# Differential attention in a two-block transformer kernel: rotation and lambda placed beside the projection, head norms in the attention loop, two weight slots filled ahead

## The chip, the cores and the metric

The kernel runs on one core of a Trainium2 chip. The metric is the device time of one execution in microseconds (us), as the median of several runs. All arithmetic here is in 32-bit floating point, but for the gather matmuls of the experts, which run on bf16 parts.

## The reference

Two transformer blocks of two layers each work on 256 tokens of width 1024, with 256 context tokens beside them. The part that the change touches is layer 1 of the first block, and the expert layers of the same block.

```python
# mixer_c: differential attention, 8 heads, each of two components of width 64
q, k, v = split(concat(ux, uc) @ c_w_qkv)          # 1024 columns each; q of the 256 tokens alone
q, k = rope(q), rope(k)                            # the 256 tokens of x; context rows are not rotated
lam = exp(sum(lq1 * lk1)) - exp(sum(lq2 * lk2)) + lam_init        # one per head
a = softmax(q1 @ k1.T / 8) - lam * softmax(q2 @ k2.T / 8)
o = a @ v                                          # 128 columns per head
o = o * rsqrt(mean(o * o) + eps) * c_subln_g * (1 - lam_init)     # head norm
y = o @ c_w_out
# hier_moe: 32 experts of width 512, the best two of a group per token
y = sum_over_two(weight * (silu(z @ w_gate[e]) * (z @ w_up[e])) @ w_down[e])
```

## The kernel before

The whole program is written out as a row of stages. A stage (`with self.stage()`) gives each engine its own list of instructions, and the next stage begins on every engine once all have come to the end of their lists. Semaphores order the engines inside a stage. An issued DMA does not hold up a stage's end unless an engine waits for it.

**Weights.** One plan lists all weight pieces in the order of their use. They go through a ring of six slots of 1 MB in SBUF, and SyncE (SP) issues a piece as soon as the slot's last user is done (`feed`, L270 to L279). A transfer issued by SP, ScalarE or GpSimd (POOL) goes to that engine's own queue, and all queues share the 16 DMA engines.

**The projection of layer 1** is `st_linear_hosting` (L385 to L495). TensorE makes 20 groups of 128 rows by 512 columns: chunks 0 and 1 are the queries of two row tiles (groups 0 to 3), chunks 2 and 3 the keys of four tiles (4 to 11), chunks 4 and 5 the values (12 to 19). ScalarE copies the even groups from PSUM (L473), VectorE the odd ones (L490); TensorE waits for the copy of group g − 6 before group g. After each group it works on one or two pieces of the conditioning vectors (`ada_w`, L414), which have nothing to do with attention: 32 pieces in four rounds. VectorE adds a round's bias (L495) and GpSimd writes it to a scratch in HBM (L465). The stage's GpSimd list ends with a wait for the last of these writes (L466). At its start VectorE finishes the residual rows of the layer before and GpSimd moves them between partitions (L454).

**The rest of the attention layer** is `mixer_c` (L1898 to L1970): a stage for the rotation and lambda (L1908 to L1940), two stages of transposes on TensorE (`st_transpose`, L510 to L551), the attention (`st_attention`, L1774 to L1895), a stage for the head norms (L1953 to L1967) and a stage of transposes. The attention runs over 16 units (8 heads, two row tiles). In unit i VectorE finds the maxima of the scores (L1836, L1838), ScalarE makes the exponentials and their sums (L1873), VectorE mixes the two components (L1847 to L1854), TensorE transposes the mix (L1805), ScalarE copies it (L1881), TensorE multiplies with the values (L1813), and ScalarE copies the result (L1885). VectorE's order is mix(i), then maxima(i + 2); mix(i) waits for the output copy of unit i − 2.

**The expert layers** are `moe` (L1115 to L1334) and `experts` (L1336 to L1545). A first stage makes the output projection of attention, the norm, the routing and its tables. Its SP list is the feed of the last four of six ring slots, which come free when that projection is done. Then `experts` runs 16 pairs of experts, and after them the pairs that hold surplus tokens. A pair takes twelve pieces of 1 MB: six go to the ring, six to spare places (two in `actT`, four in the arena). The first six spare pieces are issued when this stage begins (L1425 to L1426), later pieces as soon as the matmuls of a place are done. This is done for four row tiles in layer 0 and for two in layer 1.

Of the kernel before, what the change touches and what calls it, by code (L numbers as in the profile page):

```python
# [168 lines left out]
class Program:  # L169
    def __init__(self, nc, ctx, I, out):  # L170
# [7 lines left out]
        def count(name):  # L178
# [35 lines left out]
            "second_part", "logits_done", "m_ready", "counted", "exp_in", "exp_out", "x_normed", "x_unmixed", "row_scaled", "taps_turned", "taps_in", "gated", "conv_done", "vec_in", "bias_in", "x_in", "mods_in", "ada_bias", "ada_done", "ada_added", "ada_stored",  # L214
# [170 lines left out]
    def st_linear_hosting(self, lhsT, chunks, dest, rounds, unmix=None):  # L385
# [19 lines left out]
        with self.stage() as block:  # L405
# [37 lines left out]
            @block.sync  # L443
            def _(sp):
                self.feed(sp)
                if unmix is not None:
                    self.load_mod(sp, 1, 2, 6, (0,))

            @block.gpsimd
            def _(pool):  # L450
                if unmix is not None:
                    pool.wait_ge(sm["x_normed"].sem, sm["x_normed"].at(1))
                    for t in range(4):
                        pool.dma_start(unmix[64 * (t % 2):64 * (t % 2) + 64, (t // 2) * D:(t // 2 + 1) * D],  # L454
                                       self.xres[0:64, t * D:(t + 1) * D]).then_inc(sm["x_unmixed"].up(16), 16)
                for n, (l, r) in enumerate(rounds):
# [13 lines left out]
            def _(act):  # L470
                for g in range(0, len(groups), 2):
                    act.wait_ge(self.pe_done.sem, self.pe_done.at(g + 1))
                    nc.scalar.activation(dest(*groups[g]), self.bank[g % 6][:, :], ACT.Copy).then_inc(self.act_done.up(), 1)  # L473

            @block.vector
            def _(dve):
# [7 lines left out]
                for g in range(len(groups)):  # L484
# [630 lines left out]
    def moe(self, layer, nt):  # L1115
# [20 lines left out]
        with self.stage() as block:  # L1136
# [50 lines left out]
            def _(sp):  # L1187
                self.feed(sp)
# [147 lines left out]
    def experts(self, layer, nt, part, at):  # L1336
# [22 lines left out]
        with self.stage() as block:  # L1359
# [56 lines left out]
            def _(sp):  # L1416
# [8 lines left out]
                for m in range(R, 2 * R):  # L1425
# [348 lines left out]
    def st_attention(self, n, ncomp, operands, value, scale, dv, out_at, P0, lam=None):  # L1774
# [3 lines left out]
        nc, A, sm, bank = self.nc, self.A, self.sem, self.bank  # L1778
# [9 lines left out]
        with self.stage() as block:  # L1788
# [39 lines left out]
            def _(dve):  # L1828
# [27 lines left out]

                maxima(0)
                maxima(1)
                for i in range(n):
                    mix(i)  # L1860
                    if i + 2 < n:
                        maxima(i + 2)

# [34 lines left out]
    def mixer_c(self):  # L1898
# [6 lines left out]
        self.st_linear_hosting(lambda m, k: self.actT[:, k * T + m * P:k * T + m * P + P], C_CHUNKS, dest, C_ROUNDS, unmix=A(XX, 2048))  # L1905
        LQ = XX + 2048 + 256
        LAM = LQ + 2048
        with self.stage() as block:  # L1908
            @block.gpsimd
            def _(pool):  # L1910
                self.load_params(pool, [(A(XX, 256).rearrange("p (t n) -> p t n", t=2), I["k_rope_c"].rearrange("(t p) n -> p t n", p=P))] +
                                 [(A(LQ + 512 * i, 512), rows_to_all(I[n][0].rearrange("h d -> (h d)"), 512))
                                  for i, n in enumerate(("c_lq1", "c_lk1", "c_lq2", "c_lk2"))])

            @block.sync
            def _(sp):
                self.load_mod(sp, 2, 0, 2, (0,))

            @block.vector
            def _(dve):  # L1920
                link = self.linker(dve, self.dve_chain)
                dve.wait_ge(self.params_in.sem, self.params_in.at(80))
                for base in (QR, K):
                    for t in range(2):
                        link(self.rope(link, A(base + t * D, D), 16, 64, 64, 16, A(XX + 128 * t, 64), A(XX + 128 * t + 64, 64),
                                       A(XX + 256, 2048)))

                for i in range(2):
# [4 lines left out]
                ins.then_inc(self.dve_done.up(), 1)  # L1933
                dve.wait_ge(self.act_done.sem, self.act_done.at(1))
                nc.vector.scalar_tensor_tensor(A(LAM, 8), A(LAM, 8), LAM_INIT, A(LAM + 8, 8), ALU.add, ALU.subtract)

            @block.scalar
# [462 lines left out]
```

## Time and profile before

| | |
|---|---|
| median of the three runs | 3023.14 us (3021.97 to 3024.15) |
| profiled execution, its own time | 3028.02 us |
| span of the profiled execution | 3026.2 us |
| mean granted TensorE clock | 0.910 |
| TensorE busy | 2434.4 us, 80% |
| VectorE busy | 655.3 us, 22% |
| ScalarE busy | 368.0 us, 12% |
| GpSimd busy | 121.1 us, 4% |
| moved by DMA | 724.54 MB, mean 239 GB/s |

Times in the rows are in us from the span's start. TensorE's busy share is high over the whole span, but the touched stages lie one behind the other, and in each another thing ends last. So the place to read is the timeline of each stage, with what ended the idle time ahead of an instruction, which stands in brackets after it. The projection of layer 1 lies at 1212 to 1399, the rotation at 1399 to 1431, the attention at 1443 to 1509, the head norms at 1509 to 1522, and the two expert loops at 601 to 1158 and 1575 to 2072.

### The profile page before, as it was taken

Reading aid. Unit: us, or ns where it says so; the run is one execution under the profiler, and the core shown is the slowest. Engines: PE = TensorE matmul, PEld = TensorE weight load, DVE = VectorE, ACT = ScalarE, POOL = GpSimd, SP = SyncE. Lnnn points to the kernel's source line nnn. Section 1 sums busy time; section 2 is a strip of 40 time slices with the busy share of each in tenths; the row PEclk is TensorE's granted clock in tenths of the full one; section 3 lists DMA queues with packets and bytes.
Section 4 is the critical chain, followed back from the end, with each engine's and each line's share of the span. In section 5 each row is a group of like instructions: output and inputs, shape, how many; then the busy total and the mean of one; then the engine's idle time right before and its main releaser. Section 6 shows DMA issues by size and latency. Waiting matters only on the chain. (4 is left out here: it accounts for less than half of the span.)

```text
span 3026.2 us, 35279 instructions
## 1 busy us (share of the span) xinstructions
PE 2434.4 (80%) x14539; PEld 1323.5 (44%) x14539; DVE 655.3 (22%) x1418; ACT 368.0 (12%) x647; POOL 121.1 (4%) x166
## 2 busy tenths in 40 slices
PE   7999665899888883994668888884737999785998
PEld 3333443444343432332443333332424777563776
DVE  2000235631000004102752200003153100253000
ACT  0000121211111111000411101011013000210000
POOL 0000001000000001000010000001010000000000
PEclk9999866899999996997979999997879999897999
DMA  7787600199999995675039999995221344422442
GB/s 272 296 302 289 210 12 23 71 417 422 423 422 423 422 421 213 239 264 203 7 142 421 423 423 423 423 422 227 95 75 63 117 153 152 143 70 70 152 152 78
DMA packets 180355, 724.54 MB, mean 239 GB/s; under 512 B 14469, under 2 KB 72709, under 8 KB 114480
## 3 DMA queue, kind: packets, MB, share of 16 engines
q1 hardware_dynamic: 165824, 676.24, 57.5%
q0 software_dynamic: 8656, 25.83, 2.7%
q10 hardware_dynamic: 5792, 21.32, 1.8%
q8 instruction: 57, 0.93, 0.1%
q14 instruction: 26, 0.21, 0.0%
HBM read 699.04 MB, written 23.25 MB: 239 GB/s over the span
## 5 line engine op out<-in xcount | busy, mean ns | idle before, releaser
L1770 PE MATMUL bank<-ring,arena 128*64 128x512 f32 x1632 | 380.4, 616 | 71.5 <-DMA ring<-moe_w_up 47.1
L433 PE MATMUL bank<-ring,actT 128*128 128x512 f32 x768 | 347.0, 605 | 4.8 <-DMA ring<-c_w_qkv 2.4
L2145 PE MATMUL bank<-actT,ring 128*128 128x256 f32 x1408 | 307.3, 379 | 2.2 <-PEq L517 2.2
L2145 PEld LDWEIGHTS bank<-actT,ring 128*128 128x128 f32 x1408 | 267.4, 190 | 46.9 <-issue 11.6
L1400 PE MATMUL bank<-arena 128*64 128x512 f32 x1088 | 241.2, 595 | 27.0 <-ACT arena L1468 23.3
L1770 PEld LDWEIGHTS bank<-ring,arena 128*64 128x64 f32 x1632 | 116.2, 141 | 330.2 <-issue 217.2
L433 PEld LDWEIGHTS bank<-ring,actT 128*128 128x128 f32 x768 | 143.6, 192 | 207.8 <-issue 207.8
L549 PE MATMUL bank<-misc,arena 128*128 128x128 f32 (+1 forms) x278 | 52.8, 370 | 175.7 <-PEq L1976 53.5
L1759 PEld LDWEIGHTS bank<-arena 128*128 128x128 bf16 x5280 | 160.8, 99 | 34.2 <-issue 29.3
L1759 PE MATMUL bank<-arena 128*128 128x64 bf16 x5280 | 165.2, 195 | 5.9 <-DVE arena L1500 4.3
L1508 DVE TENSOR_TENSOR arena<-arena,bank 128x512 f32<-128x512 f32 x34 | 23.4, 688 | 663.3 <-ACT arena L1466 663.3
L2159 PE MATMUL bank<-ring,arena 128*128 128x512 f32 x352 | 154.3, 592 | 0.0
L1770 PE MATMUL bank<-actT,arena 128*64 128x512 f32 x544 | 123.7, 595 | 35.0 <-DMA actT<-moe_w_up 35.0
L1400 PEld LDWEIGHTS bank<-arena 128*64 128x64 f32 x1088 | 75.2, 137 | 171.1 <-issue 139.7
L549 PEld LDWEIGHTS bank<-misc,arena 128*128 128x128 f32 (+1 forms) x278 | 47.5, 195 | 183.9 <-issue 175.1
L331 PE MATMUL bank<-ring,actT 128*128 128x512 f32 (+2 forms) x256 | 101.5, 560 | 14.8 <-PEq L2273 12.7
L2191 DVE TENSOR_TENSOR arena<-arena,bank 128x512 f32<-128x512 f32 x22 | 15.1, 688 | 416.3 <-ACT arena L2182 416.3
L2159 PEld LDWEIGHTS bank<-ring,arena 128*128 128x128 f32 x352 | 66.9, 190 | 75.7 <-issue 74.6
L490 DVE COPY arena<-bank 128x512 f32<-128x512 f32 x24 | 16.6, 692 | 363.5 <-PE bank L433 363.5
L1770 PEld LDWEIGHTS bank<-actT,arena 128*64 128x64 f32 x544 | 41.7, 137 | 115.5 <-issue 115.5
L1150 PE MATMUL bank<-ring,actT 128*128 128x512 f32 x192 | 85.1, 604 | 2.2 <-PEq L517 2.2
L414 PE MATMUL bank<-ring,scx 128*32 128x512 f32 x704 | 85.5, 599 | 0.0
(343 smaller groups left out, 1957.3 us busy)
## 6 DMA issues: line engine op xcount, KB each, us to landing
ring<-moe_w_gate SPq DMA_DIRECT2D x136, 1024.0 KB, 24.0
arena<-moe_w_down SPq DMA_DIRECT2D x136, 1024.0 KB, 21.6
ring<-ada_w SPq DMA_DIRECT2D x96, 1024.0 KB, 7.1
ring<-moe_w_up SPq DMA_DIRECT2D x68, 1024.0 KB, 23.9
actT<-moe_w_up SPq DMA_DIRECT2D x68, 1024.0 KB, 24.7
ring<-ffn_w SPq DMA_DIRECT2D x66, 1024.0 KB, 5.2
made_scratch<-arena ACTq DMA_DIRECT2D x34, 512.0 KB, 7.8
ring<-ab_w_in SPq DMA_DIRECT2D x14, 1024.0 KB, 8.2
```

What stands on the lines that cost most here:

```text
L331: mm = nc.tensor.matmul(self.bank[bank][:, 0:ncols], lhsT(m, kt + k), sl[:, k, 0:ncols], start=(kt + k == 0), stop=(kt + k == kts - 1))
L414: mm = nc.tensor.matmul(self.bank[6 + n % 2][32 * j:32 * j + 32, :], self.scx[:, 256 * (l // 2) + 32 * k:256 * (l // 2) + 32 * k + 32], sl ...
L433: mm = nc.tensor.matmul(self.bank[g % 6][:, :], lhsT(m, k), halves[k // 4][:, k % 4, :], start=(k == 0), stop=(k == KT - 1))
L490: nc.vector.tensor_copy(dest(*groups[g]), self.bank[g % 6][:, :]).then_inc(self.dve_done.up(), 1)
L549: mm = nc.tensor.transpose(self.bank[n][0:bw, q * P:(q + 1) * P], src(t)[:, k * bw:(k + 1) * bw], self.ident)
L1150: mm = nc.tensor.matmul(proj_bank(t, c)[:, :], tok(t, 4 * j + k), halves[c][j][:, k, :], start=(j == 0 and k == 0), stop=(j == 1 and k == 3))
L1400: mm = nc.tensor.matmul(bank[4 + half][64 * i:64 * i + 64, :], A(HT + P * (2 * j + f) + S * i, S), w[:, f, half * 512:(half + 1) * 512], s ...
L1508: V_.tensor_tensor(A(HH, 512).rearrange("p (j f q) -> p j f q", f=2, q=P), self.by_rows(A(SG, 512)), self.by_rows(bank[1][:, :]), ALU.mult ...
L1759: mm = self.nc.tensor.matmul(bank[:, S * k:S * (k + 1)], part(i)[:, t * D + k * P:t * D + (k + 1) * P], pick[:, S * t:S * (t + 1)], start= ...
L1770: return self.nc.tensor.matmul(self.bank[j // 2][64 * i:64 * i + 64, :], xs[:, S * kt:S * kt + S], piece[:, k * DE:(k + 1) * DE], start=(k ...
L2145: mm = nc.tensor.matmul(bank[2 * (j % 2) + which][:, f * SEQ:(f + 1) * SEQ], w[:, k, f * P:(f + 1) * P], self.actT[:, k * T:k * T + SEQ], ...
L2159: mm = nc.tensor.matmul(bank[4 + 2 * t + half][:, :], A(H + 512 * (j % 2) + f * SEQ + t * P, P), w[:, f, half * 512:(half + 1) * 512], sta ...
```

## The change

The rotation of queries and keys and the making of lambda leave their own stage and become a part of the projection stage: GpSimd's queue gets the five table loads behind its four moves of residual rows, VectorE rotates the two query tiles after groups 4 and 5 and the two key tiles after groups 12 and 13, makes the products and sums for lambda after group 14, and ScalarE their exponentials after group 16. The load of modulation rows moves to the end of the projection's SP list. The head norms leave their own stage too: VectorE takes the statistics of unit i − 3 behind maxima(i + 2), GpSimd makes the powers in two portions (12 and 4 units), and VectorE scales 12 units after the last mix and 4 at the end. In both expert layers two spare pieces, of the first pair's down weights, are issued at the start of the first stage and not of the expert stage.

```diff
-    def st_linear_hosting(self, lhsT, chunks, dest, rounds, unmix=None):
+    def st_linear_hosting(self, lhsT, chunks, dest, rounds, unmix=None, beside=None):
...
                 self.feed(sp)
                 if unmix is not None:
                     self.load_mod(sp, 1, 2, 6, (0,))
+                    self.load_mod(sp, 2, 0, 2, (0,))
...
+                if beside is not None:
+                    beside["pool"](pool)
                 for n, (l, r) in enumerate(rounds):
...
+                    if beside is not None and g == 16:
+                        beside["act"](act)
...
+                    if beside is not None:
+                        beside["dve"](dve, link, g)
...
             @block.sync
             def _(sp):
+                first_pair = self.pair_sources(layer, 0)
+                for n in range(2):
+                    src, k, _ = first_pair[R + 2 + n]
+                    sp.dma_start(A(OVW + n * SLOT, SLOT).rearrange("p (k n) -> p k n", k=k), src).then_inc(self.spare_in[layer][2 + n], 16)
                 self.feed(sp)
                 sp.wait_ge(self.cleared, 16)
...
-                for m in range(R, 2 * R):
+                for m in (R, R + 1, R + 4, R + 5):
                     load_main(m, first[m])
...
+                def measure(i):
+                    dve.wait_ge(o_out.sem, o_out.at(i + 1))
+                    link(nc.vector.bn_stats(stat[:, 192 + 6 * i:198 + 6 * i], out_at(i)))
+                    nc.vector.bn_aggr(stat[:, 64 + 2 * i:66 + 2 * i], stat[:, 192 + 6 * i:198 + 6 * i])
...
                 maxima(0)
                 maxima(1)
+                if gain is not None:
+                    dve.wait_ge(self.params_in.sem, self.params_in.at(16))
+                    nc.vector.tensor_scalar(A(gain[0], D), A(gain[0], D), 1.0 - LAM_INIT, None, ALU.mult)
                 for i in range(n):
                     mix(i)
                     if i + 2 < n:
                         maxima(i + 2)
+                    if gain is not None and i >= 3:
+                        measure(i - 3)
+                    if gain is not None and i == n - 2:
+                        squares(0, n - 4)
+                if gain is not None:
+                    dve.wait_ge(self.pool_done.sem, self.pool_done.at(1))
+                    for i in range(n - 4):
+                        scaled(i)
+                    for i in range(n - 3, n):
+                        measure(i)
+                    squares(n - 4, n)
+                    dve.wait_ge(self.pool_done.sem, self.pool_done.at(2))
+                    for i in range(n - 4, n):
+                        scaled(i)
...
+        def turn_angles(dve, link, g):
+
+            rotate = {4: (QR, 0), 5: (QR, 1), 12: (K, 0), 13: (K, 1)}
+            if g in rotate:
+                base, t = rotate[g]
+                if g in (4, 12):
+                    dve.wait_ge(self.params_in.sem, self.params_in.at(80))
+                    dve.wait_ge(self.act_done.sem, self.act_done.at(g // 2))
+                    dve.wait_ge(self.dve_done.sem, self.dve_done.at(g // 2))
+                link(self.rope(link, A(base + t * D, D), 16, 64, 64, 16, A(TABLE + 128 * t, 64), A(TABLE + 128 * t + 64, 64), A(TMP, 2048)))
```

VectorE in the first half of the projection. Here `COPY arena<-bank` is the copy of an odd group, `TENSOR_TENSOR scx<-bank,scx` the bias add, and `COPY xres<-arena` the residual rows. Before:

```order
L490 COPY arena<-bank 128x512 x2
L495 TENSOR_TENSOR scx<-bank,scx 128x512
L490 COPY arena<-bank 128x512 x2
L487 COPY xres<-arena 128x2048
L490 COPY arena<-bank 128x512
```

and now:

```order
L495 COPY arena<-bank 128x512 x2
L500 TENSOR_TENSOR scx<-bank,scx 128x512
L738 TENSOR_TENSOR arena<-arena 128x1024
L742 TENSOR_TENSOR arena<-arena 128x32x16 x2
L744 TENSOR_TENSOR arena<-arena 128x1024
L495 COPY arena<-bank 128x512
L738 TENSOR_TENSOR arena<-arena 128x1024
L742 TENSOR_TENSOR arena<-arena 128x32x16 x2
L744 TENSOR_TENSOR arena<-arena 128x1024
L495 COPY arena<-bank 128x512
L492 COPY xres<-arena 128x2048
```

Two rotations (L738 to L744) have come between the bias add and the residual rows, one on either side of the copy of group 5.

VectorE at the end of the attention loop, from the mix of unit 15 on (`RECIPROCAL` is its first instruction). Before:

```order
L1847 RECIPROCAL stat<-stat 128x2
L1852 TENSOR_TENSOR stat<-stat,arena 128x1
L1853 TENSOR_SCALAR arena<-arena,stat 128x512
L1854 SCALAR_TENSOR_TENSOR arena<-arena,stat 128x512
L1788 UNCONDITIONAL_BRANCH
L1959 UNCONDITIONAL_BRANCH
L592 BN_STATS stat<-arena 128x6 x16
L595 BN_AGGR stat<-stat 128x2 x16
```

and now, from the statistics ahead of that mix on:

```order
L1878 MEMSET stat 128x1
L1879 TENSOR_TENSOR stat<-stat 128x12
L1880 SCALAR_TENSOR_TENSOR stat<-stat 128x12
L1858 RECIPROCAL stat<-stat 128x2
L1863 TENSOR_TENSOR stat<-stat,arena 128x1
L1864 TENSOR_SCALAR arena<-arena,stat 128x512
L1865 SCALAR_TENSOR_TENSOR arena<-arena,stat 128x512
L1872 BN_STATS stat<-arena 128x6
L1873 BN_AGGR stat<-stat 128x2
L1883 SCALAR_TENSOR_TENSOR arena<-arena,stat 128x128 x12
L1872 BN_STATS stat<-arena 128x6
L1873 BN_AGGR stat<-stat 128x2
```

The sixteen statistics of the next stage have become single pairs, and twelve scalings follow the mix.

## Rows read from the trace of the kernel before

**Rows 1.** Timeline of the rotation stage: start, length, engine, line, operation, [idle before]
```profile
1392.19 1.14 POOL L465 DMA_DIRECT2D mods_scratch<-scx  x2 [34.75 <-DVE scx L495]
1398.98 1.28 ACT L1940 ACT_TABLE_LOAD   x1 [18.05 <-PEq L405]
...
1412.85 1.22 DVE L731 TENSOR_TENSOR arena<-arena 128x1024 f32<-128x1024 f32 x1 [20.95 <-DMA arena<-c_lk]
...
1431.16 3.65 PE L549 MATMUL bank<-misc,arena 128*128 128x128 f32 x16 [40.10 <-PEq L1908]
```

**Rows 2.** Timeline of the projection stage
```profile
1234.81 8.80 PE L433 MATMUL bank<-ring,actT 128*128 128x512 f32 x16 [2.41 <-DMA ring<-c_w_qkv]
...
1262.59 0.69 DVE L495 TENSOR_TENSOR scx<-bank,scx 128x512 f32<-128x512 f32 x1 [10.19 <-PE bank L414]
```

**Rows 3.** DMA issues, KB each and us to landing; the first two issued 1221 to 1229
```profile
ring<-c_w_qkv SPq DMA_DIRECT2D x1, 1024.0 KB, 11.1
scx<-ada_b POOLq DMA_DIRECT2D x4, 64.0 KB, 8.8
...
arena<-c_subln_g POOLq DMA_DIRECT2D x1, 512.0 KB, 3.9
```

**Rows 4.** Busy time by stretch: PE, PEld, DVE, ACT, POOL, clock, DMA share, GB/s
```profile
1230.00:1234.00 4.00, 2.40 (x18) 0.42 (x16) 0.69 (x1) 0.00 (x0) 0.00 (x0) 1.00 1.07 256
```

**Rows 5.** Timeline of the attention stage
```profile
1446.98 0.17 DVE L1847 RECIPROCAL stat<-stat 128x2 f32<-128x2 f32 x1
...
1495.11 0.17 DVE L1847 RECIPROCAL stat<-stat 128x2 f32<-128x2 f32 x1 [0.65 <-ACT arena L1885]
...
1499.74 0.75 DVE L1854 SCALAR_TENSOR_TENSOR arena<-arena,stat 128x512 f32<-128x512 f32 x1
...
1502.82 0.17 DVE L1847 RECIPROCAL stat<-stat 128x2 f32<-128x2 f32 x1 [2.32 <-ACT arena L1885]
...
1508.90 0.28 ACT L1885 ACTIVATE arena<-bank 128x128 f32<-128x128 f32 x1 [1.22 <-PE bank L1813]
```

**Rows 6.** Timeline of the head norm stage
```profile
1511.86 0.86 DVE L592 BATCH_NORM_STATS2 stat<-arena 128x6 f32<-128x128 f32 x4
1512.76 1.17 DVE L595 BATCH_NORM_AGGREGATE stat<-stat 128x2 f32<-128x6 f32 x16
...
1514.43 3.30 POOL L582 TENSOR_TENSOR stat<-stat,pw 128x16 f32<-128x16 f32 x1 [3.96 <-DVE stat L603]
1517.84 4.29 DVE L1967 SCALAR_TENSOR_TENSOR arena<-arena,stat 128x128 f32<-128x128 f32 x16 [2.89 <-POOL stat L582]
1522.51 3.43 PE L549 MATMUL bank<-misc,arena 128*128 128x128 f32 x16 [13.64 <-PEq L1953]
```

**Rows 7.** Timeline, powers of one column in two other stages
```profile
1180.70 1.27 DVE L1684 SCALAR_TENSOR_TENSOR arena<-arena 128x1024 f32<-128x1024 f32 x1
1180.87 1.53 POOL L625 TENSOR_TENSOR stat<-stat,pw 128x1 f32<-128x1 f32 x1 [8.90 <-DVE stat L1695]
...
1545.07 0.56 POOL L625 TENSOR_TENSOR stat<-stat,pw 128x1 f32<-128x1 f32 x1 [13.20 <-DVE stat L1271]
```

**Rows 8.** Expert loop of layer 1: first issues of SP, and two stretches
```profile
1574.65 0.80 SPq L1421 DMA_DIRECT2D actT<-moe_w_up  x2
...
1585.66 4.25 SPq L1421 DMA_DIRECT2D ring<-moe_w_gate  x4
...
1575.00:1580.00 5.00, 4.75 (x90) 4.75 (x91) 0.21 (x3) 0.00 (x0) 0.00 (x0) 0.50 0.86 316
1580.00:1585.00 5.00, 3.64 (x27) 1.56 (x26) 0.49 (x2) 2.37 (x3) 0.00 (x0) 0.98 1.00 421
```

**Rows 9.** Expert loop of layer 0: issues of SP
```profile
600.92 0.80 SPq L1421 DMA_DIRECT2D actT<-moe_w_up  x2
...
615.32 4.42 SPq L1421 DMA_DIRECT2D ring<-moe_w_gate  x4
...
635.96 4.26 SPq L1421 DMA_DIRECT2D arena<-moe_w_down  x4
```

More of the change, by code:

```diff
@@ L1771, in gateup_tile, with st_attention @@
                                      piece[:, k * DE:(k + 1) * DE], start=(kt == 0), stop=(kt == KT - 1))
-    def st_attention(self, n, ncomp, operands, value, scale, dv, out_at, P0, lam=None):
-        nc, A, sm, bank = self.nc, self.A, self.sem, self.bank
+    def st_attention(self, n, ncomp, operands, value, scale, dv, out_at, P0, lam=None, gain=None):
+        nc, A, sm, bank, stat = self.nc, self.A, self.sem, self.bank, self.stat
         score_done, max_done, exp_done, mix_done, turned, aT_ready, o_done, o_out = (
@@ L1862, in _ @@
                         maxima(i + 2)
+                    if gain is not None and i >= 3:
[12 more added lines that the diff above has]
+                        scaled(i)
+            @block.gpsimd
+            def _(pool):
+                if gain is not None:
+                    self.load_params(pool, [(A(gain[0], D), rows_to_all(gain[1], D))])
+                    for k, (lo, hi) in enumerate(((0, n - 4), (n - 4, n))):
+                        pool.wait_ge(sm["stat_ready"].sem, sm["stat_ready"].at(k + 1))
+                        nc.gpsimd.tensor_tensor(stat[:, 40 + lo:40 + hi], stat[:, 40 + lo:40 + hi], self.pw[:, lo:hi], ALU.pow).then_inc(self.pool_done.up(), 1)
             @block.scalar
@@ L1904, in dest, with load_tables @@
             return A(base + t * D + 512 * (c % 2), 512)
-        self.st_linear_hosting(lambda m, k: self.actT[:, k * T + m * P:k * T + m * P + P], C_CHUNKS, dest, C_ROUNDS, unmix=A(XX, 2048))
-        LQ = XX + 2048 + 256
+        TMP, TABLE = O, XX + 2048
+        LQ = TABLE + 256
         LAM = LQ + 2048
[L1908 to L1926, printed above, removed]
+        sums_in, lam_exp = self.sem["sums_in"], self.sem["lam_exp"]
+        def load_tables(pool):
+            self.load_params(pool, [(A(TABLE, 256).rearrange("p (t n) -> p t n", t=2), I["k_rope_c"].rearrange("(t p) n -> p t n", p=P))] +
+                             [(A(LQ + 512 * i, 512), rows_to_all(I[n][0].rearrange("h d -> (h d)"), 512))
+                              for i, n in enumerate(("c_lq1", "c_lk1", "c_lq2", "c_lk2"))])
+        def turn_angles(dve, link, g):
[7 more added lines that the diff above has]
+                link(self.rope(link, A(base + t * D, D), 16, 64, 64, 16, A(TABLE + 128 * t, 64), A(TABLE + 128 * t + 64, 64), A(TMP, 2048)))
+            if g == 14:
                 for i in range(2):
@@ L1949, in mixer_c @@
         self.st_attention(16, 2, operands, lambda i, j: A(V + j * D + (i // 2) * P, P), 64 ** -0.5, P,
[L1950 to L1968 removed]
+                          lambda i: A(O + (i % 2) * D + (i // 2) * P, P), 0, lambda i: A(LAM + i // 2, 1), gain=(XX, I["c_subln_g"][0]))
         self.st_transpose(lambda t: A(O + t * D, D), 2, self.put_pure)
```

42 lines of the change are left out of this document (18 added, 24 removed).

## The prediction

> **What bounds the kernel now.** The program is one chain of stages; a stage ends when every engine is through with it, so what matters is what each touched stage waits for at its end, not how busy an engine is over the span. I read the timeline around the touched stages first, then the DMA issues and the stretches around them.
>
> The rotation stage is pure waiting for TensorE. The projection's last matmuls are done by 1391; VectorE adds the last conditioning bias, and GpSimd writes it out at 1392.19. ScalarE enters the next stage at 1398.98. VectorE then stands until 1412.85 for the tables, which GpSimd's queue asked for only after the stage began, works until 1430.8, and TensorE starts the transposes at 1431.16 [rows 1]. Nothing in those 32 us needs TensorE.
>
> In the projection VectorE is nearly idle: 10.19 us before the add at 1262.59. TensorE runs without a gap but for one: it waits 2.41 us, to 1234.81, for the second half of chunk 1 [rows 2]. That weight took 11.1 us to land [rows 3], while all traffic together ran at 256 GB/s [rows 4].
>
> In the attention loop the chain is VectorE's mix, TensorE's turn and values, ScalarE's copy of the output, and the next mix, which starts after 0.65 us of idle VectorE. The last output is copied at 1508.90, plus 0.28. Before the last mix VectorE is idle for 2.32 us [rows 5].
>
> The head norms then stand alone: statistics, a power of 16 columns that takes GpSimd 3.30 us, sixteen scalings in 4.29 us, and TensorE at 1522.51 [rows 6]. That is 13.3 us after the last output.
>
> The expert loops run at the rate of the weights. In layer 1 the queues move 421 GB/s from 1580 on; the first transfers of the loop are issued at 1574.65 and flow from about 1576.25 (316 of 421 GB/s over the five us from 1575). The first refill is issued at 1585.66 [rows 8]. In layer 0 the same three points are 600.92, 615.32 and 635.96 [rows 9].
>
> **The change part by part.**
>
> *Rotation and lambda moved.* The stage disappears. TensorE can start 0.38 us after the projection stage closes (the step from the last scaling, 1517.84 plus 4.29, to 1522.51 [rows 6]), so at 1399.36 instead of 1431.16: **31.8 us** less. The last write of the conditioning, for which the projection stage waits, is neither moved nor enlarged. The second load of modulation rows, 1 MB, now stands behind the 2 MB load in the same queue and not ahead of the write. I cost it at nothing; if the write did wait for the whole MB at 421 GB/s, 2.5 us.
>
> The work itself, 17.9 us for four rotations and the lambda products [rows 1], falls behind the copies of groups 4, 5, 12, 13 and 14. Queued behind it on VectorE are those copies and the next bias add. TensorE needs a bank again six groups later, and the bias two rounds later; a rotation of some 4 us is far inside both. ScalarE gains one exponential and its table load (1.28 us, [rows 1]) after group 16, equally covered. If that cover went, each would cost its own length at most.
>
> The five table loads, 1.18 MB, move on GpSimd's queue ahead of the bias loads and beside the weight for which TensorE waits. At 256 GB/s [rows 4] these bytes take 4.6 us; that is one end. The other is 0: the bias loads of before, issued in the same place, landed after 8.8 us [rows 3], at about 1234, just as the weight did. So GpSimd's queue held its share to the end already, and a longer queue behind it takes nothing more from this weight. I take **1.0 us** lost, near the row. The weights after it are wanted at least 4 us after they land.
>
> The Trainium skill, DMA: Bandwidth & Descriptors, Queues, rings and completion order, says that each DMA engine turns from queue to queue packet by packet. By that rule alone this term would be 0 and the time 1 us lower; it is a rival below.
>
> *Head norms in the loop.* Twelve pairs of statistics instructions go in ahead of a mix. Four statistics take 0.86 us and sixteen aggregates 1.17 us back to back [rows 6]; alone, with the wait between them, I take 0.28 and 0.17, so 0.45 us against 0.65 us of idle time [rows 5]: hidden, with 0.2 us to spare. Bounds: 0, and 0.25 us in each of 12 rounds (3.0 us) if a pair costs 0.9.
>
> At the loop's start VectorE now waits for the gain and scales it, 0.69 us, before the first mix at 1446.98 [rows 5]. The load is issued some 0.4 us into the stage, so at 1443.2, and takes 3.9 us [rows 3]: the mix comes 0.9 us later. Part of that lies beside scores that are slow there; I take **0.6 us** lost, bounds 0 and 1.0.
>
> After the last output, at 1509.18, remain: one pair of statistics 0.45, three small instructions 0.45, a power of 4 columns, four scalings of 0.27 [rows 6] 1.1, hops 0.2, and the stage's end 0.4. A power of one column takes 0.56 us, of sixteen 3.30 [rows 6, 7], so about 0.18 per further column and 1.1 for four. Sum 3.7 us against 13.3: **9.6 us** less. The first twelve scalings (3.2) and the three pairs before end at 1509.05 and fit ahead of the last output, with 0.1 us to spare.
>
> The power of 12 columns, 2.6 us, starts at about 1501.5: the mix before ends at 1499.74 plus 0.75, and 0.9 us of statistics follow. It ends at 1504.1, but the last mix wants to run from 1502.82 [rows 5]. In another stage a power of one column beside a VectorE instruction with two inputs in SBUF took 1.53 us, and 0.56 with VectorE idle [rows 7]: it stood until the other was done. Whether VectorE stands as well when GpSimd was first no row shows; bounds 0 and 1.1. Being nearest to that row I take **1.0 us** lost.
>
> The Trainium skill, SBUF — State Buffer, Who interferes with whom, has this rule in both directions, and it speaks against this placing of the power. By the rule the loss is the full 1.1; with separate ports it would be 0.
>
> *Two slots early.* 2.1 MB are 5.0 us at 421 GB/s. In layer 1 the four transfers that remain (4.19 MB, 10.0 us) end at 1586.2. The refill issued at 1585.66 starts to flow 1.6 us after issue, as the first ones did, at 1587.3. So 1.1 us of queue stand idle, and **3.9 us** are won, which the loop keeps since it is bound by the queue to its end. In layer 0 the queue of before ends its six slots at 602.5 plus 14.9, so 617.4, and the four pairs of refills at 637.3; the next refill, issued at 635.96, can flow only from 637.6 [rows 9]. From there both kernels are at the same point: **0 us**, bounds 0 and 0.5. The parameters that GpSimd loads beside the early slots come up to 5.0 us later; TensorE wants them only after its first tile and VectorE's results only after its second, so I cost that at nothing, and at those 5.0 us if the cover were gone.
>
> **The sum.** 31.8 − 1.0 + 9.6 − 0.6 − 1.0 + 3.9 + 0 = 42.7 us less. The profiled execution took 3028.0 us around a span of 3026.2, and becomes 2985.3; it lies 4.9 above the median of the runs, 3023.1, which becomes **2980.4 us**.
>
> **The rivals.**
> 1. *The table loads hold up the weights.* The term is 4.6 instead of 1.0: 2984.0. For it speaks the low rate at that point, against it that the GpSimd queue was busy to the end already. Chance 0.12.
> 2. *Turns by packet.* The term is 0: 2979.4. For it the 8.8 and the 11.1 us. Chance 0.2; this is the skill's rule on queues named above.
> 3. *VectorE becomes the bound of the attention loop.* A pair costs 0.9 us: 2983.4. Its cover is only 0.2 us. Chance 0.12.
> 4. *The early slots change nothing*, because the loop in layer 1 has slack after all: 2984.3. Against it stands the steady 421 GB/s. Chance 0.05.
> 5. *Slower than before:* VectorE stands at group 4 for the tables, and behind it the copies of groups 5, 7 and 9. TensorE stops at group 11, at about 1313 (an estimate: six groups of some 8.5 us after the add of group 4 [rows 2]), when it wants the bank of group 5. Each us that the tables come after that costs one. It exceeds the 42.7 us won if they land after 1356, some 130 us after their issue; landed at 1400, for instance, they give 3067. Before, they were there 13 us after theirs [rows 1]. Chance 0.01.
> 6. *The overlap does not come about*, for instance since the stage's end waits for something else just as long: about 3012. Nothing in the rows names such a thing. Chance 0.02.
>
> My forecast as it stands has 0.48. It and rivals 1 to 4 lie within 5 us of each other. All good ends together (0 for the tables, 0 for the start and for the block, 5.5 for the slots) give 3023.1 − 46.9 = 2976.2; all bad ends (4.6, 3.0 in the loop, 1.0, 1.1, 0 for the slots) 2991.4. The range is 2974 to 2992 with a little for run against run. About 0.2% of the time, 6 us, is what a measurement of this kernel can tell from no change. Faster by more 0.98, within it 0.01, slower 0.01.
>
> **What would show it.** Right: TensorE's transposes begin less than 9 us after the last conditioning matmul; its wait at chunk 1 is near 3.4 us; the round of the loop stays what it was; after the last output less than 4.5 us pass to the transposes; in layer 1 the first wait of the experts comes later and the loop ends 3.9 us sooner in itself, in layer 0 not. Wrong: a wait of TensorE for a copy or a bias in the projection, a round that has grown by more than 0.1 us, a last mix with a hole while GpSimd works (the block, if over 1.1 us), or a projection stage that closes later than 8 us after TensorE.

## The result, and the profile after

The changed kernel takes **2983.1 us** (median of 4 runs, 2981.3 to 2984.9), the kernel before 3023.2 beside it. The ratio is 0.9867, with a 95% interval of 0.985 to 0.9885: 40.1 us less, where 42.7 less and a median of 2980.4 were forecast. The profiled execution of the changed kernel took 2981.3 us around a span of 2979.4, at a mean granted clock of 0.917.

The timeline at the end of the projection and at the transposes, where the rotation stage stood before [rows 1] (line numbers are now those of the changed kernel, some 10 higher):

```profile
1388.90 1.92 PE L414 MATMUL bank<-ring,scx 128*32 128x512 f32 x16
...
1390.97 0.69 DVE L500 TENSOR_TENSOR scx<-bank,scx 128x512 f32<-128x512 f32 x1 [1.26 <-PE bank L414]
...
1391.58 0.16 DVE L1987 SCALAR_TENSOR_TENSOR arena<-arena 128x8 f32<-128x8 f32 x1
1391.95 1.17 POOL L468 DMA_DIRECT2D mods_scratch<-scx  x2 [34.76 <-DVE scx L500]
1398.62 3.65 PE L556 MATMUL bank<-misc,arena 128*128 128x128 f32 x16 [7.79 <-PEq L405]
```

The rotation is off the path: 7.8 us after its last conditioning matmul TensorE transposes, instead of 40.1. What is left is the write of the conditioning, issued at 1391.95.

TensorE at the head of the projection, answering to rows 2:

```profile
1212.71 7.11 PE L433 MATMUL bank<-ring,actT 128*128 128x512 f32 x16 [1.14 <-PEq L1640]
...
1229.66 7.13 PE L433 MATMUL bank<-ring,actT 128*128 128x512 f32 x16
1241.65 1.83 PE L414 MATMUL bank<-ring,scx 128*32 128x512 f32 x8 [4.86 <-DMA ring<-ada_w]
1243.41 8.02 PE L433 MATMUL bank<-ring,actT 128*128 128x512 f32 x16
```

The wait for the second half of chunk 1 has gone, and a wait of twice its length for a conditioning weight stands behind it.

The attention loop and its end, answering to rows 5 and 6:

```profile
1412.18 0.69 DVE L1889 TENSOR_SCALAR arena<-arena 128x1024 f32<-128x1024 f32 x1
1412.79 0.16 DVE L1858 RECIPROCAL stat<-stat 128x2 f32<-128x2 f32 x1
...
1459.62 0.28 DVE L1872 BATCH_NORM_STATS2 stat<-arena 128x6 f32<-128x128 f32 x1
...
1459.94 0.18 DVE L1873 BATCH_NORM_AGGREGATE stat<-stat 128x2 f32<-128x6 f32 x1
...
1460.36 0.17 DVE L1858 RECIPROCAL stat<-stat 128x2 f32<-128x2 f32 x1 [0.24 <-ACT arena L1938]
...
1466.67 2.29 POOL L1915 TENSOR_TENSOR stat<-stat,pw 128x12 f32<-128x12 f32 x1 [57.52 <-DVE stat L1880]
...
1468.31 0.49 DVE L1864 TENSOR_SCALAR arena<-arena,stat 128x512 f32<-128x512 f32 x1
1468.83 0.75 DVE L1865 SCALAR_TENSOR_TENSOR arena<-arena,stat 128x512 f32<-128x512 f32 x1
...
1474.15 0.28 ACT L1938 ACTIVATE arena<-bank 128x128 f32<-128x128 f32 x1 [1.38 <-PE bank L1824]
...
1475.45 1.01 POOL L1915 TENSOR_TENSOR stat<-stat,pw 128x4 f32<-128x4 f32 x1 [6.49 <-DVE stat L1880]
1476.50 1.14 DVE L1883 SCALAR_TENSOR_TENSOR arena<-arena,stat 128x128 f32<-128x128 f32 x4 [1.13 <-POOL stat L1915]
1478.02 3.27 PE L556 MATMUL bank<-misc,arena 128*128 128x128 f32 x16 [3.90 <-PEq L1799]
```

The pair of statistics has eaten 0.41 of the 0.65 us of idle time ahead of a mix, and the round is still 3.72 us. The last mix keeps its usual 0.49 and 0.75 us. Of these two only the first lies under the power of 12 columns, which ends at 1468.96; the second overlaps it by 0.13 us. From the last output to the transposes it is 3.6 us.

The same stretches in the profiles of all kernels say more than two profiles do, since TensorE's first group of the projection takes 10.06, 8.5 to 8.8, or 7.11 us from run to run (granted clock 0.70, 0.82 and 1.00). The experiments behind the kernels counted here are told in the next section. Each length in us, from the start of one row of TensorE to another's:

| stretch | without the part | with it | forecast |
|---|---|---|---|
| projection, start to fifth group (first group 8.5 to 8.8 only) | 35.4 to 37.4, mean 36.1 (5 runs) | 37.7 to 39.4, mean 38.5 (6) | +1.0 |
| fifth group to the transposes | 177.3 to 177.7 (3) | 145.2 to 145.6 (7) | −31.8 |
| last mix to the final transposes | 18.9 to 19.7 (3) | 9.5 to 10.2 (9) | −9.6 |
| layer 1, first stage and experts, first row 27.70 us | 552.2 (1) | 548.2 to 548.5 (5) | −3.9 |
| the same, first row 29.3 to 30.0 us | 553.7, 554.6 (2) | 550.5 to 550.7 (5) | −3.9 |
| layer 0, start of the first stage to the projection | 697.1 to 697.8 (3) | 695.8 to 697.4 (10) | 0 |

In this table "with it" counts every kernel that has the part and leaves its stretch as it was. In its first line the part is the table loads at the head of the projection, so that kernels which load no tables, or load them late, count as without; the first line also leaves out the profiles of the kernel before (41.0 us) and of the changed kernel (40.5), whose first groups were slower and faster than the rest. What TensorE waited for weights ahead of the fifth group doesn't hang on that choice: 0 to 2.4 us, mean 0.9, in all six profiles without tables there, and 2.2 to 4.9, mean 3.2, in all seven with them. The means give −32.2 + 2.5 for the projection, −9.7 for the end of the attention, −3.7 for layer 1 and −0.4 for layer 0, less than its runs differ among themselves.

### The profile page after: what moved, and what is told of

The parts are those of the page before. It is cut to its first block and busy times, and to the rows that moved or that the text cites. A ratio compares the mean times of both kernels' runs of the same rounds, so it can differ in the third digit from the quotient of the medians.

```text
span 2979.4 us, 35260 instructions
## 1 busy us (share of the span) xinstructions
PE 2429.5 (82%) x14539; PEld 1318.3 (44%) x14539; DVE 656.6 (22%) x1422; ACT 368.0 (12%) x647; POOL 121.5 (4%) x167
## 5 line engine op out<-in xcount | busy, mean ns | idle before, releaser
L331 PE MATMUL bank<-ring,actT 128*128 128x512 f32 (+2 forms) x256 | 101.4, 560 | 15.1 <-PEq L2307 12.7
```

The costliest lines, as they stand in the source:

```text
L331: mm = nc.tensor.matmul(self.bank[bank][:, 0:ncols], lhsT(m, kt + k), sl[:, k, 0:ncols], start=(kt + k == 0), stop=(kt + k == kts - 1))
```

## The experiments

Ten kernels and the changed one once more were run, in three lots. Each lot had its own runs of the kernel before: medians 3024.1, 3022.5 and 3021.9 us.

**The three parts alone.** Each is the kernel before with one part of the change.

```diff
 # e1_rotation: the rotation stage goes into the projection; head norms and slots as before
+        self.st_linear_hosting(..., unmix=A(XX, 2048), beside=dict(pool=load_tables, dve=turn_angles, act=raise_sums))
 # e2_norms: the head norms go into the loop; rotation stage and slots as before
+        self.st_attention(16, 2, ..., gain=(XX, I["c_subln_g"][0]))
 # e3_slots: two slots early; the rest as before
-                for m in range(R, 2 * R):
+                for m in (R, R + 1, R + 4, R + 5):
```

> The kernel before with the first part of the change alone: rotation and lambda under the projection, no norms in the loop, no early slots. Prediction's terms: 31.8 less, 1.0 back for the tables, so 30.8 less and 2992.3 us at a median of 3023.1. TensorE should start the transposes less than 9 us after the last conditioning matmul. If the 4.9 us that TensorE waits for a conditioning weight in the changed kernel are a new loss caused by the tables, the stages from the projection to the transposes should be about 30 us shorter and that wait should be here too; if they are not caused by them, the wait goes elsewhere with the same total.

Measured: 2995.9 us, ratio 0.9902 (0.9887 to 0.9918), so about 29.6 less. The transposes begin 7.6 us after TensorE's last conditioning matmul. From the projection's start to the transposes it is 183.6 us, against 214.0 and 212.8 in the two runs with the old rotation stage and a like first group: 29.8 less. TensorE waits 2.10 us for a conditioning weight and 0.79 for one of the projection: the wait comes with the tables.

> The kernel before with the head norms in the attention loop alone. Prediction's terms: 9.6 less, 0.6 back for the gain at the start, 1.0 back for the block of the last mix: 8.0 less, 3015.1 us. By the trace of the changed kernel, where neither the block nor a longer round shows: 9.8 less, 3013.3 us. If the last mix is blocked here by the power of 12 columns, its four instructions take over 2.4 us in all; if not, 1.6 as elsewhere in the loop.

Measured: 3015.9 us, ratio 0.9973 (0.9963 to 0.9982), 8.2 less. The interval spans 5.4 to 11.2, so both sums of the expectation, 8.0 and 9.8, lie in it. The last mix was not blocked: its four instructions start at 1496.18 and end at 1497.85. But the power of 12 columns ended at 1496.54, before either large instruction of the mix began, so this run does not test the block. The mix starts late here, after 2.02 us, for another reason, which the rows ahead of it show:

```profile
1493.87 1.87 PE L1819 MATMUL bank<-arena 128*128 128x128 f32 x8
...
1495.78 0.28 ACT L1933 ACTIVATE arena<-bank 128x128 f32<-128x128 f32 x1 [1.11 <-PE bank L1819]
1496.18 0.17 DVE L1853 RECIPROCAL stat<-stat 128x2 f32<-128x2 f32 x1 [2.02 <-ACT arena L1933]
```

The values of a unit take TensorE 1.06 us elsewhere in the loop and 1.87 here, where the granted clock is 0.53, so almost throughout its lower level of 1.2 GHz. The round before this mix is 0.81 us longer than usual, which is just that difference. ScalarE's copy waits for them, and the mix for the copy.

> The kernel before with the two spare slots filled early alone. Prediction: 3.9 less in the loop of layer 1, nothing in layer 0: 3019.2 us. Rival: nothing at all, 3023.1, if the loop of layer 1 has slack. Rival: both loops gain, 3.9 twice, 3015.3. The loop lengths tell it: layer 1 from 552.2 to 548.3, layer 0 unchanged at 539.4 but for the clock.

Measured: 3019.3 us, ratio 0.9986 (0.9977 to 0.9995), 4.2 less. Layer 1, measured as in the table, took 548.2 us, layer 0 697.2 against 697.8, 697.5 and 697.1 in the three kernels without early slots. So the gain is in layer 1 alone; both rivals of this run fall.

**Doubling the pair, and loading GpSimd.**

```diff
 # e6_pair_twice: a second bn_stats and bn_aggr of the same unit in the 12 rounds
...
+                    if i < n - 4:
+                        link(nc.vector.bn_stats(stat[:, 192 + 6 * i:198 + 6 * i], out_at(i)))
+                        nc.vector.bn_aggr(stat[:, 64 + 2 * i:66 + 2 * i], stat[:, 192 + 6 * i:198 + 6 * i])
 # e7_powers_beside: at the head of GpSimd's list in the attention stage
+                    for at in (96, 144, 288, 336):
+                        nc.gpsimd.tensor_tensor(stat[:, at:at + 48], self.ones[:, 0:48], self.pw[:, 0:48], ALU.pow)
```

> The changed kernel with the pair of statistics instructions done twice in each of the 12 rounds that have it. A pair takes 0.29 + 0.18 us with its wait, and 0.24 us of VectorE's idle time ahead of the mix are left beside it. Theory: the cover is that idle time and nothing more, so each round grows by 0.25 to 0.3 us, the attention stage by 3.0 to 3.6, 2986.4 us. Rival: the round is set elsewhere (ScalarE, TensorE) and takes it: no growth, 2983.1.

Measured: 2984.6 us, ratio 0.9882 (0.9865 to 0.9898). The time can't tell 3 us from none against 2983.1, but the timeline can, and shows 2.6 in all: the round is 3.95 or 3.96 us instead of 3.72 in the eleven rounds that hold a doubled pair between two mixes, and VectorE has no idle time ahead of the mix any more.

```profile
1458.09 0.18 DVE L1876 BATCH_NORM_AGGREGATE stat<-stat 128x2 f32<-128x6 f32 x1
1458.20 0.17 DVE L1858 RECIPROCAL stat<-stat 128x2 f32<-128x2 f32 x1
...
1462.15 0.17 DVE L1858 RECIPROCAL stat<-stat 128x2 f32<-128x2 f32 x1
```

So the cover of the statistics was the idle time before the mix and nothing else, and with one pair 0.24 us of it were left.

> The changed kernel with four powers of 48 columns on GpSimd (results not used) during the first half of the attention loop, some 8 us each. Theory, from the last mix of the changed kernel, whose instructions ran at their usual 0.49 and 0.75 us beside a power: a power that is under way doesn't block VectorE, the round stays 3.72 us. Rival, the rule that either engine blocks the other on instructions with two inputs in SBUF: the mixes under a power stand up to 8 us, the loop grows by 10 us or more. For the other direction: if VectorE blocks GpSimd, a power of 48 takes longer than the 8 us that 0.18 a column gives.

Measured: one time, 2983.5 us. GpSimd was busy with powers for 32 us of the loop, and VectorE took no notice:

```profile
1408.18 32.37 POOL L1914 TENSOR_TENSOR stat<-misc,pw 128x48 f32<-128x48 f32 x4
...
1418.74 0.17 DVE L1858 RECIPROCAL stat<-stat 128x2 f32<-128x2 f32 x1 [0.65 <-ACT arena L1940]
...
1419.14 0.48 DVE L1864 TENSOR_SCALAR arena<-arena,stat 128x512 f32<-128x512 f32 x1
1419.66 0.75 DVE L1865 SCALAR_TENSOR_TENSOR arena<-arena,stat 128x512 f32<-128x512 f32 x1
...
1422.46 0.17 DVE L1858 RECIPROCAL stat<-stat 128x2 f32<-128x2 f32 x1 [0.65 <-ACT arena L1940]
```

The round is 3.72 us. The powers take 8.1 us each, less than the 9.1 that the line through 0.56 us for one column and 3.30 for 16 [rows 6, 7] gives for 48. All mixes under them keep 0.48 or 0.49 and 0.75 us. This is the run that tests the block: neither engine held up the other here.

**The tables.**

```diff
 # e8_no_tables: the five loads and the wait for them are gone; rotation and lambda use what lies there
+            return
             self.load_params(pool, [(A(TABLE, 256)...
-                    dve.wait_ge(self.params_in.sem, self.params_in.at(80))
 # e4_tables_late: the loads behind the first write of the conditioning, Q rotated after groups 8 and 10
-                if beside is not None:
-                    beside["pool"](pool)
                 for n, (l, r) in enumerate(rounds):
...
+                    if beside is not None and n == 0:
+                        beside["pool"](pool)
-            rotate = {4: (QR, 0), 5: (QR, 1), 12: (K, 0), 13: (K, 1)}
+            rotate = {8: (QR, 0), 10: (QR, 1), 12: (K, 0), 13: (K, 1)}
```

> The changed kernel without the five table loads (rotation and lambda go on over whatever lies in their place; VectorE no longer waits for them). So far TensorE reaches the fifth group of the value projection 38.4 to 38.65 us after the stage's start wherever tables are loaded, whether its first group took 7.1, 8.6 or 8.7 us, and 39.2 in the kernel before, where that group took 10.1. Theory: with tables the weights bound this stretch, and without them TensorE's own work does: the fifth group comes at 36.3 plus what the first group takes over 7.1, so 0.5 to 2.4 us are won; 2981.5 us if 1.5. Prediction's term: 1.0. Rival 1: 4.6 won, 2978.5. Rival 2: nothing won, 2983.1.

Two numbers of this text are misread: in the first profiles of the kernels before and after the fifth group starts at 41.0 and 40.5 us, not at 39.2 and 38.65. The other runs stand as quoted. Measured: 2979.3 us, ratio 0.9857 (0.9841 to 0.9874). The time alone does not tell it from the changed kernel's 0.9867 (0.985 to 0.9885), the timeline does. TensorE has not one wait for a weight between 1215 and 1252 and reaches the fifth group after 35.4 us, against 38.5 on the mean with tables.

> The changed kernel with the tables loaded behind the first write of the conditioning, some 40 us later, and Q rotated after groups 8 and 10. Theory: the stretch to the fifth group is as without tables, and the tables then lie where the queues have more room: 0.5 to 2.4 us less than the changed kernel, about 2981.5. Rival: the loads cost the same wherever they are, since the whole stage runs at the rate of its weights: 2983.1, with waits of TensorE for weights later on. Second rival: the next conditioning bias, which now stands behind the tables on GpSimd's queue, comes late and TensorE waits for the bank of round 2: slower.

Measured: 2979.1 us, ratio 0.9864 (0.9848 to 0.9881), and again no wait:

```profile
1212.81 8.55 PE L433 MATMUL bank<-ring,actT 128*128 128x512 f32 x16 [1.14 <-PEq L1640]
...
1231.20 7.13 PE L433 MATMUL bank<-ring,actT 128*128 128x512 f32 x16
1238.26 1.07 PE L414 MATMUL bank<-ring,scx 128*32 128x512 f32 x8
1239.26 7.13 PE L433 MATMUL bank<-ring,actT 128*128 128x512 f32 x16
```

The fifth group comes after 35.4 us and the transposes 145.2 later, as everywhere: some 40 us on, the same loads cost nothing.

**The wait at the end, and the gain.**

```diff
 # e5_wait_moved: the wait for the last conditioning write, from the projection's list to the attention's
-                pool.wait_ge(ada_stored.sem, ada_stored.total)
+                if beside is None:
+                    pool.wait_ge(ada_stored.sem, ada_stored.total)
...
                 if gain is not None:
+                    pool.wait_ge(sm["ada_stored"].sem, sm["ada_stored"].total)
                     self.load_params(pool, [(A(gain[0], D), rows_to_all(gain[1], D))])
 # e10_wait_gain: that, and the gain scaled by GpSimd; VectorE waits for it with the first power
-                    dve.wait_ge(self.params_in.sem, self.params_in.at(16))
-                    nc.vector.tensor_scalar(A(gain[0], D), A(gain[0], D), 1.0 - LAM_INIT, None, ALU.mult)
...
+                    pool.wait_ge(self.params_in.sem, self.params_in.at(16))
+                    nc.gpsimd.tensor_scalar(A(gain[0], D), A(gain[0], D), 1.0 - LAM_INIT, None, ALU.mult).then_inc(self.pool_done.up(), 1)
 # e9_best: that, and the tables late. e11_as_changed: the changed kernel again
```

> The changed kernel, with the wait for the last write of the conditioning moved from the end of the projection stage to the head of the list of GpSimd in the attention stage. Theory: that write alone holds the stage open; VectorE's add ended at 1391.6 in the changed kernel and TensorE started at 1398.6. With the wait gone TensorE starts about 2 us after the add, 5 us less: 2978 us. The loop starts 10 us later, when the write has landed, so nothing is paid there. Rival: something else (the second load of modulation rows, a drain of the queue at the stage's end) holds the stage as long: no difference, 2983 us.

Measured: 2976.0 us, ratio 0.9842 (0.9829 to 0.9856): 7 less than the changed kernel's first runs, 5 less than its second ones below. Of that the touched stretch shows only part: from the projection's start to the final transposes it is 261.8 us here and 263.4 and 265.3 in the two profiles of the changed kernel. The wait was what held the stage open, and its removal brought a new one:

```profile
1388.98 0.69 DVE L501 TENSOR_TENSOR scx<-bank,scx 128x512 f32<-128x512 f32 x1 [1.26 <-PE bank L414]
...
1390.72 1.94 PE L557 MATMUL bank<-misc,arena 128*128 128x128 f32 x16 [1.87 <-PEq L405]
...
1398.97 0.56 POOL L293 DMA_DIRECT2D arena<-c_subln_g  x1 [7.84 <-SPq L1800]
...
1407.88 0.69 DVE L1890 TENSOR_SCALAR arena<-arena 128x1024 f32<-128x1024 f32 x1 [5.29 <-DMA arena<-c_subln_g]
```

(The wait stood at L467 of the kernel before; the description ahead says L466.) TensorE starts 1.7 us after the start of the add, against 7.4 to 7.9 in the kernels that wait there, and transposes at full speed. But the attention stage now begins some 10 us sooner, and GpSimd issues the gain with it, 0.4 us into the stage as before. The moved wait costs nothing: the two writes landed 5.5 us after their issue at 1389.97, ahead of the stage at 1398.54. What has changed is what else is under way: from 1399 to 1408 the queues moved 408 GB/s, with the loads of modulation rows that SP issued at 1389 to 1390 landing 16 and 19 us later, while in the changed kernel they moved 146 GB/s behind the issue of the gain. So the gain takes 8.9 us to land where it took 3.6 to 4.0, and VectorE stands 5.3 us before the first mix. That this traffic is the cause is argued from these rates, not tried. "Nothing is paid there" was wrong.

> The changed kernel as it is, once more, as the reference on this chip for the two below: 2983 us. Its first group of the value projection tells how this run's clock fell; with that group at 8.5 to 8.8 us the fifth group should come 37.7 to 39.1 us after the stage's start, as in the runs that had tables before it, and not at 40.5 as in its first profile.

Measured: 2980.7 us, ratio 0.9871 (0.9855 to 0.9886). First group 8.59 us, fifth group at 38.3, as expected.

> The wait for the last conditioning write moved to the attention stage, as before, and the gain scaled on GpSimd, so that VectorE needs it only for the first scaling at the loop's end. In the run with the wait alone, TensorE started 6 us sooner, but the gain came 8.9 us after its issue and the first mix began 9.95 us after the stage's start, against 4.6 to 5.0. Theory: the first mix goes back to 4.2 us, the stage from 76.2 to about 69.5, and the time from 2976.0 to 2970. Rival: the scaling on GpSimd comes late or slows VectorE's loop: the round is over 3.72 us while it runs, and the stage stays near 76.

Measured: 2973.2 us, ratio 0.9837 (0.9823 to 0.985), 7.5 below the run above it. The first mix begins 4.2 us after the stage's start and the stage takes 69.3 us. GpSimd scales the gain in 2.80 us from 1409.99 on. The two rounds around it take 3.92 and 4.13 us, 0.6 over the usual together. The first of them is longer in other kernels too, 4.2 to 4.8 us in four of them, where TensorE's scores run at the lower clock. The second is 3.7 in every kernel but this one and the next, and here GpSimd is the cause:

```profile
1409.99 2.80 POOL L1913 TENSOR_SCALAR arena<-arena 128x1024 f32<-128x1024 f32 x1 [8.29 <-DMA arena<-c_subln_g]
...
1412.17 0.90 DVE L1865 TENSOR_SCALAR arena<-arena,stat 128x512 f32<-128x512 f32 x1
```

The instruction of VectorE that usually takes 0.49 us takes 0.90 and ends 0.28 us after GpSimd's. In the next kernel the same pair takes 0.77 us and ends 0.29 after it. So a multiplication of GpSimd that is under way does hold up VectorE, by 0.4 and 0.3 us here.

> All three edits together: tables behind the first conditioning write, the wait moved, the gain scaled on GpSimd. Theory: the projection stage has no wait for weights (fifth group at 35.4 us where the first takes 8.6), 2.7 us less than the one above, 2967 us, 16 below the changed kernel. Rival: the gains share the same cover and the sum falls short; then one of the three stretches (start to fifth group, last add to transposes, first mix) does not have the length it had alone: 35.4, 1.7 and 4.2 us.

Measured: 2971.1 us, ratio 0.9833 (0.9819 to 0.9846): the fastest kernel of the study, 9.6 below the changed one on the same chip and not the 16 expected. Last add to transposes and first mix are as expected, 1.7 and 4.2 us. The fifth group is not: 37.4 us instead of 35.4, though no table is on its way. TensorE waits 1.85 us for a weight of the projection ahead of its third group, where the kernel before waited 2.41 [rows 2] and the kernel with the norms alone 0.28. So late tables remove most of the wait on the mean, but in some runs a weight is late without them. Whether late tables are worth anything on top of the other two edits, 2973.2 against 2971.1, these runs don't settle. The rest of the 16 was a sum against 2983.1, while the changed kernel stood at 2980.7 on this chip.

## Why the prediction was right

The time lay 2.7 us from the forecast, inside the range; faster was forecast with 0.98. The main terms are right for the reasons given; that the total comes as near as it does is partly luck, as the sum below shows.

- **Rotation off the path, −31.8: right.** Fifth group to transposes is 32.2 us shorter. The closing hop was 6.67 us from GpSimd's write where 7.17 was reckoned. The second modulation load, costed at nothing, cost nothing: that hop was 6.79 before [rows 1]. No copy or bias made TensorE wait.
- **Table loads, +1.0: the term that was mis-sized.** They cost 2.5 us on the mean, between the 1.0 taken and the 4.6 of rival 1. The step that failed is "GpSimd's queue held its share to the end already, and a longer queue behind it takes nothing more from this weight". It looked at this weight, chunk 1, which indeed came in time; the bytes were taken from the two behind it, for which "at least 4 us" of cover had been claimed. No row stood behind that claim, and the kernel with the norms alone, which has no tables there, waits 0.28, 0.24 and 0.33 us for three weights in a row: they land just in time, with no cover at all. By the rule that each DMA engine turns from queue to queue packet by packet (the Trainium skill, DMA: Bandwidth & Descriptors, Queues, rings and completion order) the term was to be 0. The runs don't speak against the turning, but against what I drew from it: if queues take turns, a queue with more packets keeps its turns for longer, and a weight issued meanwhile pays. That is the reading that fits: all queues together moved 227 to 244 GB/s from 1226 to 1235 in the changed kernel and 362 or less up to 1244, where the kernel before moved 401 from 1234 to 1237 and 421 after. No run shows the turns themselves.
- **The pair of statistics, 0: right**, and for the reason given. 0.41 of the 0.65 us are used; doubled, it costs 0.23 a round. Rival 3 was one pair away.
- **The gain at the loop's start, +0.6: right on the mean, and not for one reason.** The first mix comes 4.6 to 5.0 us after the stage's start instead of 4.2, and the next follows after 3.0 instead of 3.4 to 3.5: some 0.2 lost. The third follows after 3.7 us in four kernels, as without the part, but after 4.4 to 4.8 in three, where TensorE runs at its lower clock. From the stage's start to the third mix it is 11.2 to 11.4 us in the 3 profiles without the part and 11.3 to 12.7, mean 11.9, in the 7 with it. Whether the gain brings on the longer rounds is open.
- **The block of the last mix, +1.0: wrong.** The step was to take the row of a power that had run long beside VectorE [rows 7] as its mirror image. A power under way slows no instruction of VectorE, neither at 12 columns nor during 32 us of powers of 48. So the rule of the Trainium skill (SBUF — State Buffer, Who interferes with whom), that the engine that comes second stands until the first is done, does not hold for a power that came first. For the other pairs it agrees with these traces: GpSimd's multiplication of 1024 columns did hold up VectorE by 0.3 and 0.4 us, and VectorE's two-input instruction held up the powers of rows 7 by 1 us. The last round before this mix did grow, by 0.3 us on the mean (3.7 to 4.1 us, mean 3.9, in the 3 profiles without the part; 3.7 to 5.0, mean 4.25, in the 9 that have it with single pairs). With the norms alone and with the tables late, 4.5 and 4.9 us, TensorE ran in it at a granted clock of 0.53 and 0.50.
- **After the last output, −9.6: right.** 3.6 us where 3.7 were summed, and 9.7 between the means of the table. The cover ahead of it, twelve scalings and three pairs "with 0.1 us to spare", is there only while TensorE is slow enough: in four kernels, among them the one with the wait moved, the last output comes 4.5 to 5.8 us after the last mix begins. There VectorE works without a gap and sets the end: the transposes begin 9.5 us after that mix in all four.
- **The slots, −3.9 and 0: right**, alone and with the rest. In the changed kernel the first wait of the experts for a weight comes 127.8 us into the layer, in the one before 113.1:

```profile
1610.23 3.65 PE L1411 MATMUL bank<-arena 128*64 128x512 f32 x16 [1.74 <-DMA arena<-moe_w_down]
```

The parameters that GpSimd loads beside them land 12.2 us after the stage's start instead of 8.4, within the cover named.

The sum of what was measured, −32.2 + 2.5 + 0.6 − 9.7 + 0.3 − 3.7, is −42.2 us. So two errors, tables too cheap by 1.5 us and a block of 1.0 that was not there, nearly cancelled by luck. The 40.1 us of the medians agree with it within the interval, which spans 35 to 45 us.

## What to carry to other kernels

When work is moved under another stage, its loads move too: ask not only of the transfer that is waited for now, but of the ones issued next, and place bulk loads where the queue that feeds the bound engine has room. When a stage's end is shortened, look at once for what the end had been hiding. Here a 6 us gain turned into a 5 us wait for a load that had gone out into quieter queues before, and came back only when its first consumer was moved to the loop's end.

## What was not expected of the hardware

- TensorE's speed after a stand. In the changed kernel the first 16 transposes, after 7.8 us of waiting, ran at half clock; with the wait moved, after 1.9 us, at full clock. The two rows, from the table of stretches (span; busy of PE, PEld, DVE, ACT, POOL; clock; DMA share; GB/s), of the changed kernel and then of the one with the wait moved:

```profile
1398.60:1402.20 3.60, 3.58 (x16) 3.27 (x16) 0.69 (x1) 1.19 (x2) 0.00 (x0) 0.50 1.03 432
```

```profile
1390.70:1392.70 2.00, 1.94 (x16) 1.72 (x16) 0.70 (x2) 1.04 (x2) 0.43 (x1) 1.00 1.03 398
```

  0.50 and 1.00 are its two levels, 1.2 and 2.4 GHz. This stage of transposes took 7.8 us instead of 9.5.
- Two profiled executions of one kernel differ by 3 us and more in places that no edit touches: the changed kernel's fifth group came at 40.5 us in one and at 38.3 in the other, its first group at full and at 0.82 of the clock. The early one waited longer for its weights. What sets the clock of that first group was not tried.
- Two writes of 8 KB to HBM, issued at 1391.95, let TensorE go only 6.7 us later.
- A power of one column stood until a VectorE instruction with two inputs in SBUF was done, where that had begun first. In the kernel before, all nine powers of one column that take 1.51 to 1.54 us [rows 7] begin 0.16 or 0.17 us into a SCALAR_TENSOR_TENSOR of 1024 columns, which takes 1.27 or 1.28, and end 0.40 to 0.43 after it. Beside statistics, which have one input, the power took its usual time. No run separates the number of inputs from the kind of instruction.

```profile
1705.64 1.28 DVE L615 BATCH_NORM_STATS2 stat<-arena 128x6 f32<-128x512 f32 x2
1705.81 0.55 POOL L625 TENSOR_TENSOR stat<-stat,pw 128x1 f32<-128x1 f32 x1 [61.22 <-DVE stat L620]
```
